# The MLP's down product of a two-layer attention block by Strassen's scheme, in matmuls of 256 columns

## What is computed

```python
for l in range(DEPTH):
    xn = rms_norm(x, attn_norm[l])
    ...
    x = x + merged @ w_out[l]
    hn = rms_norm(x, mlp_norm[l])
    x = x + jnp.square(jax.nn.relu(hn @ w_up[l])) @ w_down[l]
return rms_norm(x, final_norm)
```

## Time and profile before

| | |
|---|---|
| runs (3) | 1530.07 us median, 1529.61 to 1531.45 |
| profiled execution: span from first to last instruction | 1525.5 us |
| TensorE busy with matmuls | 1502.5 us (98%) |
| VectorE busy | 886.8 us (58%) |
| ScalarE busy | 718.2 us (47%) |
| GpSimd busy | 437.7 us (29%) |
| granted TensorE clock, mean | 0.999 |

### The profile page before, as it was taken

The page is one execution under the profiler, slowest core; times in us unless marked ns, Lnnn a source line. Parts: engine busy times, 40 slices in busy tenths (PEclk is TensorE's granted clock), DMA queues, the critical chain, the costliest instruction groups (busy, mean ns, idle before and its releaser), DMA issues.

```text
span 1525.5 us, 21251 instructions
## 1 busy us (share of the span) xinstructions
PE 1502.5 (98%) x7396; PEld 1257.8 (82%) x7396; DVE 886.8 (58%) x1531; ACT 718.2 (47%) x1308; POOL 437.7 (29%) x459
## 2 busy tenths in 40 slices
PE   8999999999999999999999999999999999999998
PEld 6888888887888888888888888888878888888886
DVE  6874866767553544535557666667575535354454
ACT  6863777874422222222367547878643212222222
POOL 1302677774020100101022036767720101010011
PEclk9999999999999999999999999999999999999999
DMA  6343221135323333333323422212333333332233
GB/s 210 98 153 121 79 84 63 43 98 174 102 93 100 94 100 95 98 95 96 98 83 125 172 67 80 76 63 63 116 127 97 97 97 97 96 96 96 96 96 111
DMA packets 43362, 154.29 MB, mean 101 GB/s; under 512 B 5440, under 2 KB 5440, under 8 KB 43280
## 3 DMA queue, kind: packets, MB, share of 16 engines
q1 hardware_dynamic: 37296, 133.77, 27.8%
q0 software_dynamic: 5696, 18.94, 3.5%
q10 hardware_dynamic: 288, 0.52, 0.1%
HBM read 142.73 MB, written 10.49 MB: 100 GB/s over the span
## 4 chain that ended last, share of the span: by engine, by line
PE 86%; DVE 4%; ACT 4%; issue 3%; DMA 1%; POOL 1%; POOLq 0%; DVEq 0%; SPq 0%; ACTq 0%
PE G L1472 14%; PE G L1474 13%; PE G L1473 13%; PE O L1474 9%; PE O L1473 9%; PE O L1472 9%; PE O L1762 3%; PE T L1738 3%; PE S L1713 2%; PE T L1472 2%; PE T L1473 2%; PE T L1474 2%; ACT F L667 1%; PE O L1547 1%; DVE F L1413 1%
## 5 line engine op out<-in xcount | busy, mean ns | idle before, releaser
L615 ACT ACTIVATE wsplit<-stage 128x1024 fp32r<-128x1024 f32 x227 | 240.2, 1058 | 602.4 <-PE G L1474 272.6
L976 DVE TENSOR_TENSOR wsplit<-stage,wsplit 128x1024 fp32r<-128x1024 f32 x180 | 262.4, 1458 | 72.9 <-ACT wsplit L615 72.7
L601 POOL TENSOR_TENSOR F<-Y 128x512 f32<-128x512 f32 x64 | 68.5, 1070 | 637.3 <-DVE Y L1430 637.3
L1472 PE MATMUL G<-xg,wsplit 128*128 128x512 f32 x576 | 231.7, 402 | 7.3 <-DVE wsplit L1002 6.9
L1473 PE MATMUL G<-xg,wsplit 128*128 128x512 f32 x576 | 225.6, 392 | 0.0
L1474 PE MATMUL G<-xg,wsplit 128*128 128x512 f32 x576 | 225.5, 391 | 0.0
L1208 DVE CUSTOM_DVE_ANT_0 F<-S,F 128x512 f32<-128x512 f32 x192 | 93.5, 487 | 98.8 <-PE S L1713 67.5
L499 POOL TENSOR_TENSOR wsplit<-stage,wsplit 128x1024 fp32r<-128x1024 f32 x46 | 111.3, 2419 | 124.4 <-ACT wsplit L615 124.2
L786 ACT ACTIVATE F<-F,nmx 128x512 f32<-128x512 f32 x192 | 107.7, 561 | 63.4 <-DVE nmx L1208 61.8
L1472 PEld LDWEIGHTS G<-xg,wsplit 128*128 128x128 f32 x576 | 108.8, 189 | 29.3 <-DVE wsplit L1002 6.9
L1474 PEld LDWEIGHTS G<-xg,wsplit 128*128 128x128 f32 x576 | 108.6, 189 | 24.0
(11 more groups left out here) (292 smaller groups left out, 3023.3 us busy)
## 6 DMA issues: line engine op xcount, KB each, us to landing
stage<-units SPq DMA_DIRECT2D x229, 512.0 KB, 3.5
stage_n<-units_n SPq DMA_DIRECT2D x20, 512.0 KB, 4.0
gates<-Y POOLq DMA_DIRECT2D x32, 256.0 KB, 2.8
E<-gates POOLq DMA_DIRECT2D x24, 256.0 KB, 3.5
F<-gates POOLq DMA_DIRECT2D x8, 256.0 KB, 4.0
x<-x_in SPq DMA_DIRECT2D x3, 512.0 KB, 6.9
rope<-tables POOLq DMA_DIRECT2D x1, 768.0 KB, 6.0
out<-F SPq DMA_DIRECT2D x3, 256.0 KB, 2.3
```

The lines of the kernel that those rows point to most:

```text
L601: pool.tensor_tensor(F[:, m % 2, :], Y[:, m % 2, :], Y[:, m % 2, :], ALU.mult)\
L615: act.activation(wslot(u)[:, 0, :], staged(u), ACT.Copy).then_inc(s_whin if u in SN else s_whi, 1)
L976: dve.tensor_tensor(wslot(u)[:, 1, :], staged(u), wslot(u)[:, 0, :], ALU.subtract)\
L1472: pe.matmul(dst, a(0), b(0), start=first, stop=False)
```

## The change

The down product of a quarter is done in Winograd's form of Strassen's scheme. Output is cut into pairs of feature tiles (a "super", s = 0..3) and two halves of 256 tokens; the contraction into pairs of hidden tiles. Each 2x2 by 2x2 product of blocks takes seven block products (`PRODUCTS`) for eight. A down unit k (k = 2s + h) holds half (h) of the contraction of super s: 7 products x 2 contraction pairs (pp) x 3 matmuls of 256 columns. Four of the seven left operands (S1 to S4) are sums of weight blocks, four of the seven right ones (T1 to T4) sums of blocks of the activations.

Who makes what: POOL squares Y into `mixed` (`full_square`), then makes T1 to T4 of a pair of hidden tiles (`mixtures`, four operations of 256 columns), and two of the four weight sums of each unit (`weight_sums`); DVE makes the other two (`second_sums`). ACT rounds the three raw weight blocks (768 columns) and the four sums (1024 columns) in two operations (`down_hi`), and DVE makes the rests in two (`down_raw_lo`, `down_sum_lo`). ACT and DVE do the same for the activations (`halves_hi`, `halves_lo`: 768 and 1024 columns per hidden pair). The results are combined by running sums: U1 is copied by ACT (`first_product`), U2, U4, U3 are made by DVE (`pair`), and POOL adds them to x over 512 columns twice (`common_sums`); DVE adds the remaining products (`pair_first`, `pair_second`). All eight PSUM banks are used, four per super (`SETS`). The weights are laid out for it on the host, and the loads on SP stay one of 512 KB per unit. In the last down of a layer the rows of the next norm come behind each super.

```diff
+A11, A12, A22, S1, S2, S3, S4 = range(7)
+B11, B22, B21, T1, T2, T3, T4 = range(7)
+
+PRODUCTS = [(A11, B11, 2, 0), (S2, T2, 2, 1), (S1, T1, 3, 0), (S3, T3, 3, 1), (A12, B21, 0, 1), (S4, B22, 0, 0),
+            (A22, T4, 1, 1)]
...
+        U2, U3, U4, U1 = upair[:, 0, :], upair[:, 1, :], kpe[:, 0:HALF], kpe[:, HALF:S]
...
+        SETS = [[G[0], G[1], O[0], O[1]], [SB[0], SB[1], TP[0], TP[1]]]
...
+                    pool.tensor_tensor(mixed[p % 2][:, 2 * (m % 2):2 * (m % 2) + 2, :], y, y, ALU.mult).then_inc(s_hsq, 1)
...
+                def mixtures(f, p):
+                    b = mixed[p % 2]
+                    b12, b11, b22, b21, t1, t2, t3, t4 = (b[:, i, :] for i in range(8))
+                    pool.wait_ge(s_hsq, l * (QUARTERS * KT) + f * KT + (2 * p + 2))
+                    pool.tensor_tensor(t1, b12, b11, ALU.subtract).then_inc(s_mixpart, 1)
+                    pool.tensor_tensor(t3, b22, b12, ALU.subtract)
+                    pool.wait_ge(s_mixpart, l * (QUARTERS * KT) + f * KT + (2 * p + 1))
+                    pool.tensor_tensor(t2, b22, t1, ALU.subtract).then_inc(s_mixpart, 1)
+                    pool.wait_ge(s_mixpart, l * (QUARTERS * KT) + f * KT + (2 * p + 2))
+                    pool.tensor_tensor(t4, b21, t2, ALU.subtract).then_inc(s_hmix, 1)
+
+                def weight_sums(f, k):
+                    w = stage[:, down_slot(k), :].rearrange("p (a n) -> p a n", a=4)
+                    down_landed(pool, l, k, f)
+                    pool.tensor_tensor(wsum[k % 2][:, 0, :], w[:, 0, :], w[:, 3, :], ALU.add)
+                    pool.tensor_tensor(wsum[k % 2][:, 2, :], w[:, 1, :], w[:, 0, :], ALU.subtract).then_inc(s_sumpart, 1)
+
+                def common_sums(f, s):
+                    pool.wait_ge(s_u, l * (QUARTERS * KT) + f * KT + (2 * s + 1))
+                    pool.tensor_tensor(x[:, 2 * s, :], x[:, 2 * s, :], kpe[:, :], ALU.add).then_inc(s_xp, 1)
+                    x2 = x[:, 2 * s + 1, :].rearrange("p (b n) -> p b n", b=2)
+                    pool.wait_ge(s_u, l * (QUARTERS * KT) + f * KT + (2 * s + 2))
+                    pool.tensor_tensor(x2, x2, U3.unsqueeze(1).broadcast_to([P, 2, HALF]), ALU.add).then_inc(s_xp, 1)
+
                 with pool.Fori(0, QUARTERS) as f:
                     for m in range(KT):
-                        pool.wait_ge(s_gfree, l * NG + f * U_QUARTER + (G_MLP + m + 1 + GFREE0))
-                        if m >= 2:
-                            pool.wait_ge(s_hlo, l * (QUARTERS * KT) + f * KT + (m - 1))
-                        pool.tensor_tensor(F[:, m % 2, :], Y[:, m % 2, :], Y[:, m % 2, :], ALU.mult)\
-                            .then_inc(s_hsq, 1)
+                        full_square(f, m)
+                        if m % 2 == 1:
+                            mixtures(f, m // 2)
+                        if m in (5, 6):
+                            weight_sums(f, m - 5)
+                    for s in range(SUPERS):
+                        for k in (2 * s + 2, 2 * s + 3):
+                            if k < KT:
+                                weight_sums(f, k)
+                        common_sums(f, s)
...
+                def down_hi(f, k):
+                    down_landed(act, l, k, f)
+                    act.wait_ge(s_wused, l * NU + f * U_QUARTER + (U_MLP + KT + k - (10 if k < 2 else 2) + 1 + WUSED0))
+                    raw = stage[:, down_slot(k), 2 * P:8 * P].rearrange("p (a b n) -> p a b n", a=3, b=2)
+                    act.activation(dsplit[:, k % 2, 0, A11:S1, :, :], raw, ACT.Copy).then_inc(s_dhi, 1)
+                    if k >= 2 and k % 2 == 0:
+                        first_product(f, k // 2 - 1)
+                    act.wait_ge(s_wsum, l * (QUARTERS * KT) + f * KT + (k + 1))
+                    act.activation(dsplit[:, k % 2, 0, S1:, :, :], wsum[k % 2].rearrange("p a (b n) -> p a b n", b=2), ACT.Copy)\
+                        .then_inc(s_whi, 1)
+
+                def first_product(f, s):
+                    act.wait_ge(s_prod, l * (QUARTERS * 3 * SUPERS) + f * (3 * SUPERS) + (3 * s + 1))
+                    if s > 0:
+                        act.wait_ge(s_xp, l * (QUARTERS * KT) + f * KT + (2 * s - 1))
+                    act.activation(U1, SETS[s % 2][2][:, 0:HALF], ACT.Copy).then_inc(s_u1, 1)
...
+                def halves_hi(f, p):
+                    act.wait_ge(s_hsq, l * (QUARTERS * KT) + f * KT + (2 * p + 2))
+                    act.activation(halves[:, 0, p, B11:T1, :], mixed[p % 2][:, 1:4, :], ACT.Copy).then_inc(s_hpart, 1)
+                    act.wait_ge(s_hmix, l * (QUARTERS * SUPERS) + f * SUPERS + (p + 1))
+                    act.activation(halves[:, 0, p, T1:, :], mixed[p % 2][:, 4:8, :], ACT.Copy).then_inc(s_hhi, 1)
...
+                        if m >= KT - 2:
+                            down_raw_lo(f, m + 2 - KT)
+                            down_sum_lo(f, m + 2 - KT)
+                        elif not (isinstance(f, int) and m == 0):
                             split_lo(l, U_MLP + m + 2, f)
...
+                        if m % 2 == 0 and m > 0:
+                            halves_lo(f, m // 2 - 1)
+                        if m in (KT - 3, KT - 2):
+                            second_sums(f, m + 3 - KT)
+                    halves_lo(f, SUPERS - 1)
+                    second_sums(f, 2)
...
+                def second_sums(f, k):
+                    w = stage[:, down_slot(k), :].rearrange("p (a n) -> p a n", a=4)
+                    at = l * (QUARTERS * KT) + f * KT + (k + 1)
+                    dve.wait_ge(s_sumpart, at)
+                    dve.tensor_tensor(wsum[k % 2][:, 1, :], wsum[k % 2][:, 0, :], w[:, 1, :], ALU.subtract).then_inc(s_sum2, 1)
+                    dve.wait_ge(s_sum2, at)
+                    dve.tensor_tensor(wsum[k % 2][:, 3, :], w[:, 2, :], wsum[k % 2][:, 1, :], ALU.subtract).then_inc(s_wsum, 1)
+
+                def down_raw_lo(f, k):
+                    dve.wait_ge(s_dhi, l * (QUARTERS * KT) + f * KT + (k + 1))
+                    raw = stage[:, down_slot(k), 2 * P:8 * P].rearrange("p (a b n) -> p a b n", a=3, b=2)
+                    dve.tensor_tensor(dsplit[:, k % 2, 1, A11:S1, :, :], raw, dsplit[:, k % 2, 0, A11:S1, :, :], ALU.subtract)
+
+                def down_sum_lo(f, k):
+                    u = U_MLP + KT + k
+                    split_rounded(dve, l, u, f)
+                    dve.tensor_tensor(dsplit[:, k % 2, 1, S1:, :, :], wsum[k % 2].rearrange("p a (b n) -> p a b n", b=2),
+                                      dsplit[:, k % 2, 0, S1:, :, :], ALU.subtract).then_inc(s_wlo[BN[u] % 2], 1)
...
+                def pair(f, s, between):
+                    b, a, c, d = SETS[s % 2]
+                    product(f, s, 1)
+                    dve.wait_ge(s_u1, l * (QUARTERS * SUPERS) + f * SUPERS + (s + 1))
+                    dve.tensor_tensor(U2, U1, c[:, HALF:S], ALU.add).then_inc(s_u2, 1)
+                    between()
+                    product(f, s, 2)
+                    dve.wait_ge(s_u2, l * (QUARTERS * SUPERS) + f * SUPERS + (s + 1))
+                    dve.tensor_tensor(U4, U2, d[:, 0:HALF], ALU.add).then_inc(s_u, 1)
+                    dve.tensor_tensor(x[:, 2 * s + 1, 0:HALF], x[:, 2 * s + 1, 0:HALF], d[:, 0:HALF], ALU.add)
+                    dve.tensor_tensor(U3, U2, d[:, HALF:S], ALU.add).then_inc(s_u, 1)
+
+                def pair_first(f, s):
+                    at = l * (QUARTERS * KT) + f * KT + 2 * s
+                    product(f, s, 3)
+                    dve.wait_ge(s_xp, at + 1)
+                    dve.tensor_tensor(x[:, 2 * s, :], x[:, 2 * s, :], SETS[s % 2][0][:, :], ALU.add).then_inc(s_gfree, 1)
+
+                def pair_second(f, s):
+                    at = l * (QUARTERS * KT) + f * KT + 2 * s
+                    dve.wait_ge(s_wused, l * NU + f * U_QUARTER + (U_MLP + KT + 2 * s + 2 + WUSED0))
+                    dve.wait_ge(s_xp, at + 2)
+                    x21 = x[:, 2 * s + 1, HALF:S]
+                    dve.tensor_tensor(x21, x21, SETS[s % 2][1][:, HALF:S], ALU.add).then_inc(s_gfree, 1)
...
+                with dve.Fori(0, QUARTERS - 1) as f:
+                    for s in range(SUPERS):
+                        if s < SUPERS - 1:
+                            down_raw_lo(f, 2 * s + 2)
+                            pair(f, s, lambda: down_sum_lo(f, 2 * s + 2))
+                        else:
+                            pair(f, s, lambda: split_lo(l, U_MLP + U_QUARTER, f))
+                        if s < SUPERS - 1:
+                            second_sums(f, 2 * s + 3)
+                        pair_first(f, s)
+                        pair_second(f, s)
+                        if s < SUPERS - 1:
+                            down_raw_lo(f, 2 * s + 3)
+                            down_sum_lo(f, 2 * s + 3)
+                        else:
+                            split_lo(l, U_MLP + U_QUARTER + 1, f)
+                        if s < SUPERS - 2:
+                            second_sums(f, 2 * s + 4)
...
```

(34 more changed lines are left out.)

133 lines of the change are left out of this document (98 added, 35 removed).

## The result

The changed kernel takes **1634.6 us** (median of 4 runs, 1629.3 to 1636.0) against 1530.4 for the kernel before on the same chip: ratio 1.068, 95% interval 1.066 to 1.070, 104 us slower. The forecast was 1662 with 1585 to 1710: sign, case and range held, and the time was put 27 us too high (a loss of 132 instead of 104).

A forecast was written before the change was run, and what follows sets the result against it. TensorE, busy 98% of the span, was taken as the bound. Eight quarters at 15.3 us more (122), plus 6 and 4, made 132: span 1658, median 1662 us, 8-in-10 range 1585 to 1710.

The forecast's parts named there:

- TensorE's saving, 26.9 us: Down units: 42 matmuls of 256 columns at 0.1195 us take 3.36 us less per quarter, 26.9 in all.
- GpSimd's 256 columns at 0.73: Price of a GpSimd two-input operation of 256 columns, from the line through 512 and 1024: 0.73 us.
- L646 and L647 near 0.73 us: Sign expected in the changed kernel's profile: these GpSimd operations would last near 0.73 us.
- VectorE and GpSimd exclude each other, in either order: VectorE operations with both inputs in SBUF and GpSimd's block each other; VectorE holds 1.08 us for 1024 columns, 0.82 for 768.
- No stall in the up tiles: Up tiles: TensorE never stalls, weight rests being 0.8 us early at the tightest.
- The turn, unit 2 at 21.3: From up to down tiles: late relus, rests and mixtures delay unit 2's start to 21.3 us after up tile 7.
- GpSimd's square 5 "ends at -6.9": At the turn: GpSimd's square 5 ends 6.9 us before up tile 7's end, with unit 0's sums behind it.
- the 2.5 us of wait for L1555 in unit 1, eight times: At the turn: TensorE waits 2.5 us in unit 1 for pair 3's last rest, eight times.
- The steady super, 12.5 a period and waits of 2.4 before units 3, 5, 7: Down units after the turn: odd units start every 12.5 us instead of 10.04, TensorE waiting 2.4 us before each.
- The falling clock, a rival at 1750: Rival: TensorE's clock falls after the new waits, up to 2.5 us each, 88 us more, 1750; chance 8%.
- the forecast case: Whole kernel: waits from VectorE and GpSimd meetings outweigh TensorE's saving, 1600 to 1705 us; chance 72%.
- The last downs and ends: Layer 1's last down adds 6 us for next-norm rows; adds to x at each layer's end add 2 each, 4.

The follow-up runs named there:

- e12: Kernel before with 42 matmuls of 256 columns for 24 of 512 per down tile, eighth hidden tile left out, no sums added: 1503.4 us.
- e1: Changed kernel with GpSimd's two-input MLP operations replaced by pairs of memsets that read nothing and take about as long: 1561.3 us.
- e3: Changed kernel with 16 extra matmuls of 256 columns on TensorE before the waits of down units 3, 5 and 7: 1631.5 us.
- e8: e1 with VectorE's relu of up tile 7 ahead of hidden pair 2's rests and unit 1's sums: 1543.8 us.
- e4: Changed kernel with the squares of the hidden tiles made by ScalarE instead of GpSimd: 1610.7 us.
- e6: Changed kernel with GpSimd's two adds to x per super made by VectorE: 1618.1 us.
- e5: Changed kernel with VectorE's relu of up tile 7 ahead of hidden pair 2's rests and unit 1's sums: 1627.8 us.
- e9: Changed kernel with e4, e5, e6, odd rests before adds to x, and ScalarE's square 7 ahead of its rounding for unit 1: 1583.7 us.
- e11: e9 with unit 2's rounding and last rest ahead of super 0's first product, and last downs' roundings and rests moved earlier: 1579.0 us.

## Why the forecast held, and where it was too high

- **TensorE's saving, 26.9 us:** right. e12 shows 25, with an interval of 23 to 29.
- **GpSimd's 256 columns at 0.73:** right, 0.738 alone. The sign given for it, "L646 and L647 near 0.73 us", did not come: they average 0.80 to 1.45, since they meet VectorE's work. The price was right, and the sign forgot the waiting that the forecast itself assumed for GpSimd. The Trainium skill (GPSIMD Engine Reference, Elementwise — side-by-side cycle accounting) has 4497 ns for 2048 columns; the estimate of 0.56 us worked out from it would have been too low.
- **VectorE and GpSimd exclude each other, in either order:** right, and shown by taking it away (e1: 73 us less). The holds of 1.08 and 0.82 were measured as taken.
- **No stall in the up tiles:** right. In every quarter the eight up tiles last 43.5 us.
- **The turn, unit 2 at 21.3:** this step failed by 3.0 us a quarter; it started at 18.3. The first step of its working, GpSimd's square 5 "ends at -6.9", was put too late: it ended at -8.7 (549.33 + 1.04 against 559.1). The relu of tile 6 ended at -1.9, not -0.65, the relu of tile 7 at 5.4, not 7.4, and pair 3's last rest at 14.2, not 16.9. The order of events was right, but two things on the way were not: the 2.5 us of wait for L1555 in unit 1, eight times, were 0.3 to 0.5 us, four times; and unit 1's start (11.3 against 11.8) is near the forecast partly by luck, because a fall of the clock that this case left out made unit 0 some 1.5 us longer.
- **The steady super, 12.5 a period and waits of 2.4 before units 3, 5, 7:** the waits are there (ended by L1574, 24 in all), but 1.8, 0.8 and 1.3 us in the quarter of the table; from the start of unit 2 to the end the six quarters of the loop take 36.2 on average instead of 37.5. The steps came in the order forecast, each a little early. From unit 5's start (597.12) to unit 7's (608.71) are 11.6 us:
```profile
605.64 0.67 DVE L1596 TENSOR_TENSOR x<-x,G 128x512 f32<-128x512 f32 x1
606.24 0.41 DVE L1603 TENSOR_TENSOR x<-x,G 128x256 f32<-128x256 f32 x1
606.57 0.94 DVE L1569 TENSOR_TENSOR dsplit<-stage,dsplit 128x768 fp32r<-128x768 f32 x1
607.44 1.21 DVE L1574 TENSOR_TENSOR dsplit<-E,dsplit 128x1024 fp32r<-128x1024 f32 x1
```
  The adds from PSUM end at 9.5 (forecast 10.05), the raw rest at 10.4 (10.9), the sum rest at 11.5 (12.1), and no weight sum of GpSimd came between, for which the forecast had 0.4. From unit 3 to unit 5 it is 12.6, as forecast, but 0.7 of that is luck: unit 3 ran at the lower clock, and its first product came out 0.7 us late.
- **The falling clock, a rival at 1750:** the falls came, 18 in the down units, which the forecast case left out. The one shown costs its unit 1.5 us, not 2.5, and the ten behind the turn cost nothing that could be told (e3), as they were followed by waits in any case.
- **The last downs and ends:** 6 and 4 us were added for them. The six other quarters came to +11.0 each (66 instead of 92), the two last downs, counted to TensorE's next matmul, to +18.1 and +17.2 (35 instead of 37). In the second of these 2.3 us are TensorE's wait for the last adds and rows, which the forecast had booked as an end. The 6 us left are 2.9 before the first down product (whose start lies between 456.7 and 460.7 us in the versions, so this is no effect of the scheme), 0.9 between the layers, 2.0 behind the last down and 0.2 in the up tiles. Together 107 of span instead of 132. The error lies in the turn and the steady super of the six.

From the changed kernel's 1634.6 to the 1503.4 of e12 are 131 us: the 104 lost and the 27 not won. The meetings take 73 of them (e1), the relu's place 17.5 more (e8), and 40 are left between e8 and e12: late units 1 and 2 (2.4 us a quarter, 19 in all), the last downs (4.9 and 4.4), and the rest in the steady super and the ends, which no run took apart.

## What to carry to other kernels

A scheme that trades TensorE's work for sums must be priced on the shared resource of the engines that make the sums, here the port of VectorE and GpSimd, and not on their busy shares: VectorE was free for half of the stretch and GpSimd for nine tenths, and neither share counted. Where the two take turns, taking operations with SBUF inputs away from both, to ScalarE, helped most (e4, 24 us), and moving some from GpSimd to the faster VectorE less (e6, 16.5). And a wait removed at one place of a chain that is full mostly moves to the next unit (e5, e9, e11: 17 us together where 63 to 80 were expected), so order pays only until the fuller engine is reached.

## What was not expected of the hardware

- **Strict turns.** With work on both sides, the port changed hands after each instruction in the stretch shown: a VectorE operation of 0.42 us alone took 1.1 on average, and GpSimd's of 0.74 took 1.43 to 1.70. In the kernel before only VectorE was seen waiting; GpSimd waits just as well.
- **Writes alone didn't take the port.** GpSimd's memsets ran beside VectorE's two-input operations, and these kept their bare durations (e1: 1.22, 0.95 and 0.42 us).
- **The clock can fall after short waits.** A gap of 1.96 us was followed, 0.7 us into the next unit, by 3.2 us of matmuls at the pace of 1.2 GHz; before it lay 5 us of full work and, 7 us back, a gap of 1.33 us. After a gap of 1.88 us before unit 3 in another quarter (1387.69) no fall followed: the unit took 5.11 us at a granted clock of 1.00. No run here shows what decides it.
